# The twelfth tile pair of four gated networks, from plain products to seven block products

## The reference, cut to what matters

```python
def swiglu(h, w_gate, w_up, w_down):
    return (jax.nn.silu(h @ w_gate) * (h @ w_up)) @ w_down

for i in range(DEPTH_2):                         # 2
    h = rmsnorm_2(x, ffn1_norm[i])
    x = x + FFN_HALF * swiglu(h, ffn1_w_gate[i], ffn1_w_up[i], ffn1_w_down[i])
    ...                                          # pooling (i = 0) or latent attention (i = 1)
    h = rmsnorm_2(x, ffn2_norm[i])
    x = x + FFN_HALF * swiglu(h, ffn2_w_gate[i], ffn2_w_up[i], ffn2_w_down[i])
```

## Time and profile before

| what | value |
|---|---|
| median of 3 runs | 2523.28 us (2521.16, 2523.28, 2523.41) |
| the profiled execution's own time | 2521.13 us |
| its span, first to last instruction | 2519.8 us |
| mean granted TensorE clock | 0.995 of full speed |
| TensorE matmuls busy | 98% of the span, 14234 matmuls |
| VectorE busy | 71%, 2879 instructions |
| ScalarE busy | 45%, 1987 instructions |
| weight reads | 375 DMAs of 512 KB, 3.5 us from issue to landing |

### The profile page before, as it was taken

One profiled execution on the slowest core, in us unless ns is written; L12 is line 12 of the kernel. 1 busy time (PEld: TensorE's weight loads), 2 busy tenths in 40 slices (PEclk: granted clock), 3 DMA queues, 4 the chain that ended last, 5 costly groups with the idle time before them and its releaser, 6 DMA issues. The chain is left out here.

```text
span 2519.8 us, 36066 instructions
## 1 busy us (share of the span) xinstructions
PE 2462.8 (98%) x14234; PEld 2149.4 (85%) x14234; DVE 1794.6 (71%) x2879; ACT 1145.6 (45%) x1987; POOL 397.0 (16%) x301
## 2 busy tenths in 40 slices
PE   8899999999999999999999999999999999999999
PEld 7777777888887889898889898989898888799998
DVE  5896655665635868687968687868677576787776
ACT  4486443444423435355535354535354555453433
POOL 3673402322202100002000001000001432100000
PEclk9999999999999999999999999999999999999999
DMA  5211312323222233332233333323232111232323
GB/s 173 68 50 55 104 43 67 109 92 100 90 97 71 87 101 101 101 106 83 91 102 101 101 94 107 104 90 118 77 108 84 48 51 45 91 117 100 104 81 101
DMA packets 66520, 227.75 MB, mean 90 GB/s; under 512 B 7216, under 2 KB 8752, under 8 KB 66352
## 3 DMA queue, kind: packets, MB, share of 16 engines
q1 hardware_dynamic: 66352, 225.44, 28.8%
HBM read 223.31 MB, written 2.10 MB: 89 GB/s over the span
## 5 line engine op out<-in xcount | busy, mean ns | idle before, releaser
L526 DVE TENSOR_TENSOR wl<-raw,wh 128x1024 fp32r<-128x1024 f32 (+2 forms) x511 | 502.9, 989 | 240.8 <-ACT wh L517 238.5
L517 ACT ACTIVATE wh<-raw 128x1024 fp32r<-128x1024 f32 (+2 forms) x511 | 416.0, 835 | 487.0 <-PE main L581 244.3
L645 POOL TENSOR_TENSOR acc<-acc,sq 128x512 f32<-128x512 f32 (+1 forms) x88 | 127.0, 1443 | 1274.2 <-ACT sq L640 1268.9
L579 PE MATMUL main<-hxh,wh 128*128 128x512 f32 x624 | 246.9, 396 | 7.6 <-DVE tmp L880 4.2
L581 PE MATMUL main<-hxh,wl 128*128 128x512 f32 x624 | 243.6, 390 | 0.0
L580 PE MATMUL main<-hxl,wh 128*128 128x512 f32 x624 | 243.4, 390 | 0.0
L517 ACT ACTIVATE wh<-sum 128x512 fp32r<-128x512 f32 x288 | 168.5, 622 | 94.5 <-PE score L581 47.3
L526 DVE TENSOR_TENSOR wl<-sum,wh 128x512 fp32r<-128x512 f32 x288 | 195.0, 687 | 20.5 <-ACT wh L517 18.1
L579 PEld LDWEIGHTS main<-hxh,wh 128*128 128x128 f32 x624 | 117.5, 188 | 36.5 <-DVE tmp L880 4.3
L1873 PE MATMUL score<-th,wh 128*128 128x256 f32 x504 | 143.5, 285 | 1.8 <-ACT kept L1976 1.7
L1875 PE MATMUL score<-th,wl 128*128 128x256 f32 x504 | 142.6, 283 | 0.0
(11 more groups left out here) (519 smaller groups left out, 7065.8 us busy)
## 6 DMA issues: line engine op xcount, KB each, us to landing
raw<-in_wts SPq DMA_DIRECT2D x375, 512.0 KB, 3.5
raw<-in_wts SPq DMA_DIRECT2D x52, 384.0 KB, 3.0
x<-in_xT SPq DMA_DIRECT2D x4, 512.0 KB, 7.5
out<-x SPq DMA_DIRECT2D x8, 256.0 KB, 2.0
memx<-in_memT SPq DMA_DIRECT2D x1, 1024.0 KB, 9.6
raw<-in_wts SPq DMA_DIRECT2D x4, 256.0 KB, 2.6
band<-in_pool SPq DMA_DIRECT2D x1, 768.0 KB, 4.5
rope<-in_rope SPq DMA_DIRECT2D x1, 512.0 KB, 7.1
```

What stands on the lines that cost most here:

```text
L517: e.activation(halves_of(wh, i), src, ACT.Copy).then_inc(*sig.up("weight_high", ("high", i)))
L526: e.tensor_tensor(halves_of(wl, i), src, f(halves_of(wh, i)), ALU.subtract) \
L579: e.matmul(o, ah, bh, start=start, stop=False)
L645: e.tensor_tensor(acc[:, 0:n], acc[:, 0:n], sq_turn(nm).of(("sq", nm, k))[:, 0:n], ALU.add) \
```

## The change

The set of pairs that are made in halves becomes empty. Pair 11 then takes the other way in `tile_order`, in all four networks: seven block products, with GATE_RIGHT and S4 put behind into pair 12. GATE_RIGHT and S4 of pair 10 now stand between the block products of pair 11. `weight_source`, `fetch`, `sum_weights` and the per-step functions of ScalarE and VectorE follow that order without an edit of their own; `half_product` is no longer called.

```diff
 OPENING = 3
-HALVED = (11,)
+HALVED = ()
 UP_LEFT, UP_RIGHT, S4, GATE_RIGHT, S1, S2, S3 = 1, 2, 3, 4, 5, 6, 7
```

## The result

Over 15 runs of each, the changed kernel takes 2527.31 us and the kernel before 2521.7; the ratio is 1.0022 with a 95% interval of 1.0014 to 1.003. The change makes the kernel about 5.6 us slower (3.5 to 7.6). The prediction said 4.7 us slower, 2528.0, with a range of 2524.0 to 2532.0.

A forecast was written before the change was run, and what follows sets the result against it. It took TensorE to bound plain-pair rounds and VectorE, at 10.70 us a pair, six block pairs in a row. Loss of 8.2 us less gain of 3.5 made 4.7 slower: 2523.28 + 4.7 = 2528.0 us, range 2524.0 to 2532.0.

The forecast's parts named there:

- The columns: TensorE, pair 11: 84 matmuls of 256 columns for 48 of 512 gain 0.87 us a network, 3.5 in all.
- The lag and its cap: VectorE's L2010 falls 0.63 us further behind TensorE's GATE_RIGHT per block pair, until TensorE stalls at 3.45 us.
- L(11): Lag of pair 11 from the end of GATE_RIGHT on TensorE to L2010 on VectorE: 3.44 us in f10.
- L(8): Lag of pair 8, taken as unchanged: 1.55 us in f10, 1.74 in f20, 1.98 in f11, 1.68 in f21.
- The losses: Late S3 in round 1 cost 1.87 us in f10, 2.05 in f20, 2.29 in f11, 1.99 in f21; 8.2 in all.
- The mechanism of the stall: TensorE's S3 needs ScalarE's copy of S2, which stands behind a silu waiting for VectorE's L2010: 0.54 us late.
- What the lag comes from: VectorE's 18 instructions per block pair, almost without gaps, take 10.70 us against TensorE's 10.08.
- interleave the regimes: Skill rule for a contended engine that changes over time: the plain pair was such an interleaving, so removing it loses.
- The places: Buffer ring: round 1's 53 half buffers become 56, the empty one ahead of the down products goes, at no cost.
- The sum: Whole kernel: loss 8.2 us, gain 3.5, so 4.7 slower, 2528.0 us.
- The absorbed lag: Rival, 10%: round 1 absorbs VectorE's lag, the columns' 3.5 us stay, 2519.8 us.
- late at the start of round 1: Rival, 15%: late weight reads cost 2.0 us per network hit; 6.7 us slower with one, 8.7 with two.

The follow-up runs named there:

- experiments 3, 5 and 10: In order: copy_first (3); copy_first with later buffer places as in the kernel before, 2511.72 us, ratio 0.9971 (5); weights_last (10).
- places_only: Kernel before, pair 11 still plain, one half-buffer pair skipped in round 1 so later buffers lie as in the changed kernel: 2522.58 us, ratio 1.0007.
- copy_first: Changed kernel with ScalarE reordered: silu behind the kept copy of S2, hidden rows' rounded copy behind the kept copy of S3: 2515.12 us, ratio 0.9977.
- silu_only: Changed kernel with only the silu moved behind the kept copy of S2 on ScalarE: 2515.36 us, ratio 0.9987.
- places_back: Changed kernel with three half-buffer pairs skipped in round 1, so later buffers lie as in the kernel before: 2526.13 us, ratio 1.0023.
- weights_last: copy_first with the next stage's activation split ahead of due weights at a network's last down product, on ScalarE and VectorE: 2509.36 us, ratio 0.9954.

## Why the prediction was right, and where it was not

**The columns: right.** The gain of 0.87 us a network, 3.5 in all, is what experiments 3, 5 and 10 show in round 1 (0.86 each).

**The lag and its cap: right, to a tenth.** L(11), L(12) and L(13) are 3.43 to 3.45 us in all four networks, S3 of pairs 12, 13 and 14 is late by 0.51 to 0.54, and pair 15 is free. L(8) was taken as fixed from one trace, and it is not: f10 1.55 became 1.90, f11 1.98 became 1.71, and places_only, which is the kernel before up to there, has 1.89 in f10. The losses were to be 1.87, 2.05, 2.29 and 1.99 us; they are 2.31, 2.30, 2.12 and 1.95 (the table's difference and the 0.87), 8.7 in place of 8.2.

**The mechanism of the stall: right, and shown.** With the copy ahead of the silu, no S3 is late although the lag passes 2.91 us and reaches 3.36 in f20 of copy_first and 3.82 in silu_only. The Trainium skill, "TensorE: Matmul & The Clock Gate", says in its section "Architectural detail: the array is 16× 32×32, not 1× 128×128" that ScalarE and VectorE are strict FIFO; the kept copy that waits 3.0 us behind a silu in the trace after agrees.

**What the lag comes from: wrong in part.** The prediction read the 10.70 us of a pair as VectorE being full, its instructions following "with almost no gap". The windows of one period, of the kernel before and of copy_first, say otherwise (behind the length stand the busy times of TensorE, its weight loads, and VectorE; x19 counts one instruction that reaches in from outside):

```profile
1467.26:1477.96 10.70, 10.23 (x84) 10.13 (x84) 9.84 (x19) 5.71 (x13) 0.00 (x0) 1.00 0.34 96
978.06:988.23 10.17, 10.17 (x87) 10.17 (x86) 9.76 (x19) 6.07 (x13) 0.00 (x0) 1.00 0.32 105
```

VectorE was busy for 9.84 us of the 10.70, less than TensorE's 10.08. Most of the rest were the two waits in VectorE's rows of the trace after, 0.29 us ahead of a low part and 0.42 ahead of L2001, which ScalarE's order had put there: the weight copy behind the silu, and the kept copy of S3 behind the hidden rows' copy. In copy_first the second is gone and the first is short, and a new one of 0.28 has come; without it the list would take some 9.9 us, an estimate (10.17 - 0.28). So 10.70 and 10.17 both hold waits for ScalarE, and neither is VectorE's own time. What is left of the lag grows by 0.09 a pair, and eight pairs in a row do not feel that. The plain pair was no rest that VectorE needed: it broke off the stalls that an order made. The rule of the Trainium skill that was drawn on, "Perfetto Trace Analysis", section "Optimization Strategy" (interleave the regimes), agrees with the sign of the change as it stands, where round 1 is 5.2 us longer without the plain pair, and no longer matters in copy_first, where the interleaving is gone and the columns are gained.

**The places: wrong.** The step that failed is "The 53 half buffers of round 1 become 56, so the one left empty ahead of the down products goes: no cost." It looked at round 1 only. Where the places lead at the end of the network, a weight copy had to wait for the last down product, with the split of the next stage behind it. The cost shown by places_only is 0.9 us of wait behind f10 and 0.58 us behind f20; with the clock (below) the join behind f10 is longer by some 2 us in the mean of the traces, though the two sets overlap: from f10 pair 21 to f20 pair 3, the six traces with the places of before have 112.4 to 115.2 us, mean 113.7, and the five with the changed ones and the old order of the join have 114.8 to 116.1, mean 115.5.

**The sum.** Round 1 gave 5.2 in place of 4.7 us, and the places add about 2. That is 7, at the upper end of what was measured (3.5 to 7.6). The prediction's 4.7 came out near the middle because the term that it missed is small, not because it had seen everything. That its 2528.0 lies only 0.7 us from the measured 2527.31 is partly luck: its base of three runs, 2523.28, was 1.6 above the 2521.7 of fifteen, and the change 0.9 larger than forecast.

**The rivals.** The absorbed lag is refuted by the 19 stalls. No read was late at the start of round 1 in the trace after; f21 had one at pair 18 of round 2 (lag 3.71). In places_back one hit pair 13 of f20, and its S3 of pair 14 was late by 1.21.

## What to carry to other kernels

When one engine's time per tile is read from a stretch in which the engines wait for one another, it is the time of the loop and not of the engine: count the waits inside the period, again after each mend, and look at which instruction stands in front of the one that is waited for, before calling an engine full. A copy that frees the bottleneck's buffer belongs ahead of anything that waits for a third engine. And a change in the number of pieces that pass through a ring of buffers shifts every later user of the ring: follow the places up to the next stage whose start is on the path.

## What was not expected of the hardware

The join behind f10 costs different amounts with the same waits, by the granted clock of TensorE. In the 25 us around it the mean granted clock (the column after POOL) is, for the kernel before and then for the changed one:

```profile
1157.80:1182.80 25.00, 22.14 (x153) 21.00 (x152) 19.09 (x30) 13.84 (x24) 4.43 (x4) 0.93 0.41 127
```

```profile
1158.80:1183.80 25.00, 21.26 (x125) 20.08 (x123) 13.40 (x22) 10.87 (x19) 3.57 (x3) 0.80 0.30 95
1169.80:1173.20 3.40, 3.38 (x16) 3.40 (x17) 0.84 (x2) 1.40 (x1) 0.00 (x0) 0.50 0.02 6
```

Directly behind the wait of 3.7 us the clock is at 0.50, the lower of its two levels. Of the 3.25 us by which this join is longer in the trace after, 0.9 are the wait (2.86 us before, 3.74 after), and the rest fits the clock: 0.13 less over 25 us is up to 3.3 us of TensorE's time, an estimate that counts idle time too. But the idle time alone does not fix how long the lower level lasts: places_back has the wait of 2.9 us and 0.80 over the same 25 us, places_only the wait of 3.7 and 0.86, and weights_last the wait of 1.5 and 0.86. What decides between them stayed open.
